# HGRN's input without the root in its elements, and the first two projection units run chunk by chunk while x is copied in

## The reference, cut to what matters

```
u = rmsnorm(x, norm_mix[0])            # x * rsqrt(mean(x*x) + eps) * gain
q, f, i, g = split(u @ w_in)           # 4 x 1024 columns
forget = lb + (1 - lb) * sigmoid(f);  key = 1 - forget
query = silu(q);  value = i;  log_f = log(forget)
# per head, in chunks: scores of query and key with decays from the
# running sum of log_f, a state carried from chunk to chunk,
o = rmsnorm(o, out_gain) * silu(g)
h = x + o @ w_out
```

## Time and profile before

| | |
|---|---|
| median of 3 runs | 2271.11 us (2269.19 to 2276.2) |
| the profiled execution | 2268.27 us |
| its span in the trace | 2266.5 us |
| TensorE busy (matmul) | 2180.3 us, 96% of the span |
| VectorE (DVE), ScalarE (ACT), GpSimd (POOL) busy | 1007.2, 872.8, 1175.6 us |
| mean granted clock of TensorE | 0.987 |

### The profile page before, as it was taken

How to read it: one execution, slowest core, us unless ns; L and a number is a source line. 1 busy time by engine, 2 the same in 40 slices (tenths; PEclk the granted TensorE clock), 3 DMA queues, 4 the chain that set the end, 5 groups by cost and what they waited for, 6 DMA issues and landing times. The chain is left out here.

```text
span 2266.5 us, 28352 instructions
## 1 busy us (share of the span) xinstructions
PE 2180.3 (96%) x10458; PEld 1795.5 (79%) x10458; DVE 1007.2 (44%) x1479; ACT 872.8 (39%) x1237; POOL 1175.6 (52%) x639
## 2 busy tenths in 40 slices
PE   4899999999999999989999999999899999999997
PEld 3788878888888978878888888788656888888886
DVE  5365566431434037754431446442675235422432
ACT  4567754221323223444221333434465234322222
POOL 3877855554565454535554555455113555554552
PEclk8999999999999999999999999999899999999999
DMA  3121213332332322223332332322101223332331
GB/s 135 56 65 56 74 47 93 93 109 86 95 108 85 93 85 67 72 70 102 94 112 83 93 107 88 123 63 90 56 14 51 95 93 93 100 110 80 101 104 72
DMA packets 53254, 193.30 MB, mean 85 GB/s; under 512 B 6816, under 2 KB 7728, under 8 KB 52912
## 3 DMA queue, kind: packets, MB, share of 16 engines
q1 hardware_dynamic: 50688, 184.95, 26.1%
q10 hardware_dynamic: 2480, 7.19, 0.8%
HBM read 187.92 MB, written 4.19 MB: 85 GB/s over the span
## 5 line engine op out<-in xcount | busy, mean ns | idle before, releaser
L1495 POOL TENSOR_TENSOR w_split<-ring,w_split 128x1024 fp32r<-128x1024 f32 (+3 forms) x327 | 842.9, 2578 | 857.1 <-ACT w_split L1013 857.1
L1013 ACT CAST w_split<-ring 128x1024 fp32r<-128x1024 f32 (+3 forms) x327 | 356.4, 1090 | 1018.2 <-PE ps L385 882.8
L383 PE MATMUL ps<-u_split,w_split 128*128 128x512 f32 x1768 | 705.8, 399 | 22.5 <-POOL w_split L1495 9.7
L385 PE MATMUL ps<-u_split,w_split 128*128 128x512 f32 x1768 | 693.3, 392 | 0.0
L384 PE MATMUL ps<-u_split,w_split 128*128 128x512 f32 x1768 | 692.9, 392 | 0.0
L383 PEld LDWEIGHTS ps<-u_split,w_split 128*128 128x128 f32 x1768 | 334.9, 189 | 102.0 <-issue 19.9
L385 PEld LDWEIGHTS ps<-u_split,w_split 128*128 128x128 f32 x1768 | 334.6, 189 | 71.5
L384 PEld LDWEIGHTS ps<-u_split,w_split 128*128 128x128 f32 x1768 | 335.0, 189 | 68.3 <-issue 1.2
L383 PE MATMUL ps<-hid,w_split 128*128 128x512 f32 x648 | 254.5, 393 | 4.2 <-DVE arena L1975 2.8
L384 PE MATMUL ps<-hid,w_split 128*128 128x512 f32 x648 | 253.3, 391 | 0.0
L385 PE MATMUL ps<-hid,w_split 128*128 128x512 f32 x648 | 253.1, 391 | 0.0
(11 more groups left out here) (297 smaller groups left out, 2535.6 us busy)
## 6 DMA issues: line engine op xcount, KB each, us to landing
ring<-in_w_hgrn SPq DMA_DIRECT2D x32, 512.0 KB, 3.6
ring<-in_w_attn_qk SPq DMA_DIRECT2D x24, 512.0 KB, 3.5
ring<-in_w_merge SPq DMA_DIRECT2D x24, 512.0 KB, 3.2
ring<-in_w_gu0a SPq DMA_DIRECT2D x22, 512.0 KB, 3.5
ring<-in_w_gu0b SPq DMA_DIRECT2D x22, 512.0 KB, 3.6
ring<-in_w_gu1a SPq DMA_DIRECT2D x22, 512.0 KB, 3.5
ring<-in_w_gu1b SPq DMA_DIRECT2D x22, 512.0 KB, 3.5
ring<-in_w_gu2a SPq DMA_DIRECT2D x22, 512.0 KB, 3.5
```

Source lines behind the costliest of these rows:

```text
L383: nc.tensor.matmul(ps[:, bank], ws[:, 0, r, w], act[:, 0, c], start=c == 0, stop=False)
L385: m = nc.tensor.matmul(ps[:, bank], ws[:, 1, r, w], act[:, 0, c], start=False, stop=c == n - 1)
L1013: nc.scalar.copy(ws[:, 0, slot, 0:w], ring[:, r, 0:w]).then_inc(s["w_hi"], 1)
L1495: nc.gpsimd.tensor_tensor(ws[:, 1, slot, 0:w], ring[:, r, 0:w], ws[:, 0, slot, 0:w].bitcast(F32), ALU.subtract).then_inc(s["w_lo"], 1)
```

## The change

The root is no longer in u: `first_norm` on ACT makes the high part of x times gain straight from x (Copy with a scale), `first_input` on DVE the low part, while the squares run beside. SP issues gains and lbl first, then the weights of units 0 and 1, then x with a semaphore for each pair of chunks, ones, and the rest. TensorE runs units 0 and 1 of head 0 in turn by chunks as they come, then the mean square, then goes on. The root is applied to each of the four results of every head by a product on DVE (`hgrn_raw`, from the bank to SBUF), so the sigmoids, the query and silu(g) now read SBUF, and ACT's copy of the value is gone. The third sigmoid moves beside the first two on ACT, silu(g) to behind the first masked score copy on DVE. POOL has no part of the first norm; its lists of splits and level products at the start are reordered. Some semaphores are merged (v_root and r_tok to `roots`, mix_* to `mix_steps`, rope_a_scaled to `rope_scaled`) without other work.

```diff
-            for c in range(DC):
-                sp.dma_start(h[:, c], a["x"][:, c]).then_inc(s["x_loaded"], 16)
-            for dst, name in constants[:2]:
-                sp.dma_start(dst[:], a[name]).then_inc(s["norm_consts"], 16)
...
-                    for k in range(RING):
+                    for dst, const in constants[:2]:
+                        sp.dma_start(dst[:], a[const]).then_inc(s["norm_consts"], 16)
+                    for k in range(2):
+                        sp.dma_start(ring[:, k, 0:width], w[k]).then_inc(w_ready[k], 16)
+                    for c in range(DC):
+                        sp.dma_start(h[:, c], a["x"][:, c]).then_inc(s[f"x_loaded{c // 2}"], 16)
+                    sp.dma_start(ones[:], a["ones"]).then_inc(s["norm_consts"], 16)
+                    for k in range(2, RING):
                         sp.dma_start(ring[:, k, 0:width], w[k]).then_inc(w_ready[k], 16)
...
 # TensorE
-            FREED = ("sig_f", "query", "silu_g", "vf_ready")
+            FREED = ("raw_f", "raw_q", "raw_g", "vf_ready")
...
-            pe.wait_ge(s["norm_consts"], 32)
+            for c in range(DC):
+                hgrn_project(0, 0, ready=u_chunk(0), part=(c, c + 1))
+                hgrn_project(0, 1, part=(c, c + 1))
+            pe.wait_ge(s["norm_consts"], 16 * 3)
             mean_square(0)
-            for k in range(4):
-                hgrn_project(0, k, ready=None if k else u_chunk(0))
+            for k in range(2, 4):
+                hgrn_project(0, k)
...
 # ACT
+            def first_norm():
+
+                act.wait_ge(s["norm_consts"], 16 * 2)
+                hi("hgrn", 0)
+                hi("hgrn", 1)
+                for c in range(DC):
+                    act.wait_ge(s[f"x_loaded{c // 2}"], 16 * 2)
+                    nc.scalar.activation(us[:, 0, c], h[:, c], ACT.Copy, scale=gains[:, 0, c:c + 1]).then_inc(s["u_hi"], 1)
+                    if c >= 4:
+                        act.wait_ge(s["sq_sum"], max(c - 4, 1))
+                    nc.scalar.activation(nsq[:, c % 4], h[:, c], ACT.Square).then_inc(s["sq_ready"], 1)
+                rms(0)
...
+            def hgrn_sigmoid(head, raw, src, dst, done):
+
+                act.wait_ge(s[raw], cnt(head, 1, 1))
+                nc.scalar.activation(dst, src, ACT.Sigmoid).then_inc(s[done], 1)
...
-            hgrn_sigmoid(0, 0, sf_, "sig_f")
-            hi("hgrn", 2)
-            hgrn_sigmoid(0, 1, sq_, "sig_q")
-
             act.wait_ge(s["lb_steps"], 5)
             nc.scalar.activation(lbt[:, 0:3], lbt[:, 0:3], ACT.Exp).then_inc(s["lb_steps"], 1)
+            hi("hgrn", 2)
+            hgrn_gate_sigmoids(0)
+            hi("hgrn", 3)
             hgrn_log(0)
-            hi("hgrn", 3)
+            hi("hgrn", 4)
             decay_exps(0, dec, 0)
             decay_exps(0, dec, 1)
-            hi("hgrn", 4)
             decay_exps(0, dec, 2)
+            hi("hgrn", 5)
             decay_exps(0, dec, 3)
             state_exps(0, bcum, dec, chd)
-            hi("hgrn", 5)
-            hgrn_value(0)
-            hgrn_sigmoid(0, 2, sg_, "sig_g")
...
                 if more:
-                    hgrn_sigmoid(nxt, 0, sf_, "sig_f")
-                    hgrn_sigmoid(nxt, 1, sq_, "sig_q")
+                    hgrn_gate_sigmoids(nxt)
+                hgrn_sigmoid(head, "raw_g", sgl, sg_, "sig_g")
                 act.wait_ge(s["vt_ps"], cnt(head, 1, 1))
...
-                    hgrn_value(nxt)
                     hi(*hgrn_unit(nxt2, 1)) if not isinstance(head, int) else hi("hgrn_out", 1)
-                    hgrn_sigmoid(nxt, 2, sg_, "sig_g")
...
 # POOL
-            lo("hgrn", 0)
-            norm(0, "hgrn")
-            lo("hgrn", 2)
-            lo("hgrn", 3)
-            hgrn_decayed(0, {4: lambda: lo("hgrn", 4), 8: lambda: lo("hgrn", 5)})
-            lo("hgrn", 6)
+            for k in range(5):
+                lo("hgrn", k)
+            hgrn_decayed(0, {2: lambda: lo("hgrn", 5), 5: lambda: lo("hgrn", 6)})
             lo("hgrn", 7)
...
 # DVE
+            def first_input(c):
+
+                dve.wait_ge(s["u_hi"], c + 1)
+                nc.vector.scalar_tensor_tensor(out=us[:, 1, c], in0=h[:, c], scalar=gains[:, 0, c:c + 1],
+                                               in1=us[:, 0, c].bitcast(F32), op0=ALU.mult, op1=ALU.subtract
+                                               ).then_inc(s["u_lo_odd"] if c % 2 else s["u_lo_even"], 1)
+                if c >= 2:
+                    add_square(0, c - 1)
...
+            def hgrn_raw(head, done, bank, dst):
+
+                unit = (1, 0, 2, 3).index(bank)
+                dve.wait_ge(s["w_used"], cnt(head, 4, FIRST["hgrn"] + unit + 1))
+                nc.vector.tensor_tensor(dst, ps[:, bank], rs[:], ALU.mult).then_inc(s[done], 1)
...
-                nc.vector.tensor_tensor(qry[x], sq_, ps[:, 0], ALU.mult).then_inc(s["query"], 1)
+                nc.vector.tensor_tensor(qry[x], sq_, qry[x], ALU.mult).then_inc(s["query"], 1)
...
-                nc.vector.tensor_tensor(sgl, sg_, ps[:, 2], ALU.mult).then_inc(s["silu_g"], 1)
+                nc.vector.tensor_tensor(sgl, sg_, sgl, ALU.mult).then_inc(s["silu_g"], 1)
...
-                    if n == 0:
-                        dve.wait_ge(s["scores"], cnt(head, 8, 1))
+                    if n == 1:
                         hgrn_silu(head)
...
                 if more:
                     end_exponents(bcum, dec)
+                    hgrn_raw(nxt, "vf_ready", 3, vf)
                 dve.wait_ge(s["o_lo"], cnt(head, 1, 1))
                 head_output(head, hgain, ors, otmp, sgl, otmp, s["o_full"])
+                if more:
+                    dve.wait_ge(s["o_scaled"], cnt(head, 1, 1))
+                    hgrn_raw(nxt, "raw_g", 2, sgl)
+                if not isinstance(head, int):
+                    hgrn_raw(nxt2, "raw_f", 1, sf_)
+                    output_rooted(head, ors, otmp, otmp, s["o_full"])
+                    hgrn_raw_query(nxt2)
```

More of the change, by code:

```diff
@@ L286, in program @@
         block = ctx.enter_context(nc.Block())
-        constants = ((gains, "gains"), (ones, "ones"), (ident, "ident"), (lvl_mask, "lvl_mask"), (reset, "reset"),
-                     (lbl, "lbl"), (hgain, "hgain"), (cos_a, "cos_a"), (sin_a, "sin_a"),
+        constants = ((gains, "gains"), (lbl, "lbl"), (ident, "ident"), (reset, "reset"), (lvl_mask, "lvl_mask"),
+                     (hgain, "hgain"), (cos_a, "cos_a"), (sin_a, "sin_a"),
                      (win_mask, "win_mask"), (res_mask, "res_mask"),
@@ L512, in hgrn_out @@
                 if lo == 0:
-                    pe.wait_ge(s[("query", "sig_f")[k]], HEADS_H)
+                    pe.wait_ge(s[("raw_q", "raw_f")[k]], HEADS_H)
                 unit("hgrn_out", k, hid, k, n=DC - 1, ready=lambda c: pe.wait_ge(s["o_lo"], c + 2), part=(lo, hi))
@@ L1145, in _, with hgrn_gate_sigmoids @@
             act.wait_ge(s["credit"], 2)
-            norm(0, "hgrn")
-            def hgrn_sigmoid(head, k, dst, done):
-                src = (1, 0, 2)[k]
-                act.wait_ge(s["w_used"], cnt(head, 4, FIRST["hgrn"] + k + 1))
-                if head != 0 and k:
-                    act.wait_ge(s[("", "query", "silu_g")[k]], cnt(later(head, -1), 1, 1))
-                nc.scalar.activation(dst, ps[:, src], ACT.Sigmoid).then_inc(s[done], 1)
+            first_norm()
+            def hgrn_sigmoid(head, raw, src, dst, done):
+                act.wait_ge(s[raw], cnt(head, 1, 1))
+                nc.scalar.activation(dst, src, ACT.Sigmoid).then_inc(s[done], 1)
+            def hgrn_gate_sigmoids(head):
+                hgrn_sigmoid(head, "raw_f", sf_, sf_, "sig_f")
+                hgrn_sigmoid(head, "raw_q", qry[(head if isinstance(head, int) else head[1]) % 2], sq_, "sig_q")
             def hgrn_log(head):
@@ L1819, in _ @@
             nc.vector.memset(start[:, 2:3], 0.0).then_inc(s["o_rstd"], 2)
-            for c in range(1, DC - 1):
-                add_square(0, c)
-            dve.wait_ge(s["norm_consts"], 32)
+            for c in range(DC):
+                first_input(c)
             def cumulate(it, b, log_decay):
@@ L2119, in times_sin @@
                 if x == 0:
[L2120 removed]
+                    dve.wait_ge(s["rope_scaled"], 4)
                 if x >= 2:
@@ L2346, in _ @@
             ffn(2, 7)
-            norm(7, s["credit"])
+            last_norm(7, s["credit"])
 def kernel(**inputs):
```

113 lines of the change are left out of this document (46 added, 67 removed).

## The result

Seven runs of each kernel: 2272.55 us before (2269.19 to 2277.68) and **2255.45 us after** (2253.3 to 2264.35). The ratio is 0.9928, with a 95% interval of 0.9907 to 0.9948: 17.1 us faster by the medians, where 2250 was forecast. The profiled execution of the changed kernel took 2261.79 us, its span is 2260.0.

The account below looks back on a forecast made before the run. TensorE, busy nearly all the span, was taken as the bound. Prologue -24.6 and heads +3.6 give -21.0 us: 2268.27 profiled becomes 2247.3, and the median, 2.8 above, 2250; range 2241 to 2260.

Parts of the forecast that it names:

- Steps 1 to 3: Prologue copies, weight splits and x parts: weights 0 and 1 split by 11.2 us, first low part held until then.
- Step 4: Prologue, units 0 and 1 in turn: 48 matmuls from 11.3 to 24.2 us, some 10 at 1.2 GHz.
- Step 5: Prologue, weight 2 split only after the root: TensorE waits 6.7 us, unit 2 then takes 7.4, to 40.0.
- Step 6: Prologue, units 3 to 5 run through in 16.3 us; head 0 starts at 56.3, 24.6 us gained, bounds 19 to 27.
- Head 0: First head: POOL a few microseconds behind its old place, but weights 6 and 7 and last levels still in time.
- Rival D: Heads: query and silu, reading SBUF, both stand out a POOL split; 4.6 us lost per head, 2278.7 us; chance 0.03.
- Heads 1 to 5: Head loop: scan to POOL's split 0.7 us later, less 0.1; TensorE waits 0.6 more per head, 3.6 in six.
- 0.1 of spare: Head loop: POOL ends the split about 0.1 us before TensorE starts that unit, taken off the 0.7 us delay.
- rival A: Heads: they lose nothing, as ACT's freed 3 us reach the loop and cover silu; 2245.5 us; chance 0.25.
- The sum: Whole kernel: prologue -24.6 and heads +3.6 give -21.0 us, 2250 for the median.

Follow-up runs that it names:

- second pair: Kernel before and changed kernel, unaltered, each traced once more on another chip: head 0 starts 24.3 us earlier in the changed one, the last head 16.9.
- POOL waits: Changed kernel, with POOL in head 0 waiting for the next head's key before its two end products: head 0 period 35.97 us, where it was 37.83.
- early, weight 5 too: Changed kernel, weights 2 and 3 cast before root's Ln, weight 5 cast and split earlier, POOL waiting for key in head 0: head 0 at 52.44, last head 284.39 us.
- silu between levels: Changed kernel, third sigmoid behind the log on ACT, silu between DVE's first and second pair of decay levels: head periods 35.1 to 37.1 us.
- both late: Changed kernel, third sigmoid behind the log on ACT and silu behind DVE's state chain: head period stays at 33.73 us.
- the last run: Changed kernel, weights 2 and 3 cast before root's Ln, POOL in head 0 waiting for key: 2252.96 us against 2274.97 for the kernel before, ratio 0.9911.

## Why the prediction was right, and where its steps were off

The forecast of 2250 lay 5.5 us low, inside its range. The mechanism of the start and of the later heads was the one that the trace shows; head 0 was missed, and two errors of the first steps cancelled. By its steps:

- **Steps 1 to 3** (copies, splits, x): TensorE starts at 11.03, predicted 11.3, but that is in part luck. ACT loads a table (1.28 us from 5.57) ahead of the casts, which the sum had not. The casts ended at 8.9, predicted 7.7, and POOL's splits at 10.3 and 13.1, predicted 8.6 and 11.2. The first low part was to stand out the split of weight 1 to 11.2. It stood out that of weight 0 instead and got in ahead of the other. That the gap is a matter of 0.1 us, and that TensorE starts 2.2 us later when it is missed, wasn't seen. DVE, then POOL of the changed kernel:

```profile
9.51 1.37 DVE L1702 SCALAR_TENSOR_TENSOR u_split<-arena,gains_sb,u_split 128x512 fp32r<-128x512 f32 x1 [8.42 <-ACT u_split L1046]
...
10.29 2.83 POOL L1504 TENSOR_TENSOR w_split<-ring,w_split 128x1024 fp32r<-128x1024 f32 x1
```

- **Step 4** (48 matmuls in turn): 26.07, predicted 24.2. The term mis-sized is the slow phase: 15 matmuls at 0.43 us, where 10 were reckoned from the earlier trace rows, and a wait of 0.52 for the late split of weight 1. The traces of the changed kernel and its variants have 9 to 17 slow matmuls here, so no single number would have done. From 18.46 on the matmuls are 0.23 us apart (the 47 in 10.60 us of the earlier trace rows give 0.2255, not 0.2265, a difference of no weight). The Trainium skill tells of one kernel whose cycling through banks kept bringing back the half clock (TensorE: Matmul & The Clock Gate, "A second HAM failure mode: psum-queue depth-cycling"); the trace of these turns between two banks shows no such fall after 18.46.
- **Step 5** (the hole): 6.2 us of waiting, 6.7 predicted. Unit 2 took 7.9 us, not 7.4, again by more slow matmuls.
- **Step 6** (units 3 to 5): they ran through, but for 0.37 us. Weight 4's split took 4.49 us beside DVE's level halves and ended at 47.8, predicted 43.5; the bounds had reckoned with such a split for weight 5. Head 0 at 59.0, predicted 56.3: 21.9 us gained (24.3 in the second pair), inside 19 to 27.
- **Head 0** is the step that failed. I wrote that POOL "is then a few microseconds behind its old place", and checked only whether its results come in time for TensorE. I did not ask which DVE instruction now stands beside POOL's end products and split. The forget product did: 5.41 us. Head 0 lost 4.7 us, of which 0.6 are the loss of every head and 4.1 are DVE's delay. "POOL waits" shows POOL's work beside DVE as the cause and takes 1.9 of them away; the rest moved to other instructions. Rival D described the mechanism, but for query and silu in every head.
- **Heads 1 to 5**: predicted 0.6 us each by TensorE's wait for POOL's split; measured 0.55, a wait of 0.47. The cause is also the one given. Without silu ahead of it the scan stays at +6.96, held by the log, and without silu and sigmoid it comes at +6.46. POOL's string starts 0.5 later, not 0.7, and next to nothing of the 0.1 of spare was there. The two table loads of a head that were to go went (7 to 5) and brought nothing, as said against rival A; by the periods A is out.
- **The sum**: -21.9 + 4.7 + 2.7 = -14.5 at the last head in the first pair of traces, -24.3 + 4.7 + 2.7 = -16.9 in the second, -17.1 by the medians of the whole. The forecast had -24.6 + 3.6 = -21.0: the start and head 0 make up the difference.

## What to carry to other kernels

Where one engine feeds another without slack, its whole unbroken string counts: an instruction of a third engine that slows one link by 0.5 us costs as much as a start that is 0.5 us late, so a moved instruction has to be checked against what the other engines run beside it, before and behind its new place. When a change starts a stage earlier, list what of the slower engines now falls on its first steps; the hole tends to come back a few units later. In a short prologue, what stands first in a list decides, not what lands first.

## What the runs showed of the hardware

- A DVE instruction can wait for more than one instruction of POOL: L1919, with one SBUF input, stood out four in a row (the rest of a half level, two products in 2.53, a split in 2.38), 5.41 us in all, and 0.65 where POOL waited for it. But it need not be so: in the prologue the low part issued at 9.51 was served between two splits that followed each other directly. It was done after 1.37 us, and the second split took 2.83 for 2.35. The Trainium skill (SBUF — State Buffer, "SBUF: two separate sides") says that who starts first has the pair of ports for the whole instruction; the trace agrees with that in both cases. Who gets in between two instructions of POOL stays open.
- At the first low part a few hundredths decided whether DVE got into the gap between two splits (issued at 10.10 it did, at 10.13 and 10.27 it did not); the price was 2.2 us of TensorE's start.
- In the first stretch (11.0 to 18.4 us) the profile's clock column shows 1.00 while the matmuls are 0.43 us apart. The column and the pace agree elsewhere (0.50 and 0.43 at 34 to 38 us); at the very start go by the starts of the matmuls.
- What an idle stretch of TensorE costs behind it differs from one time to the next. After 2.2 us without a matmul it ran at 1.2 GHz for 6.7 us ("early, weight 5 too"), and after 2.83 the clock fell in the kernel before. After 2.80 at the same place in the changed kernel, and after 2.38 in "silu between levels" (head at 101.21), it stayed at 1.00.
- One stretch of 650 matmul records had the clock at 1.00 and 111.8 us in one execution ("both late"), 0.90 and 122.3 us in another of nearly the same program (the last run). The 10.5 us between them are as much as the changed kernel's fastest and slowest runs differ by; which stretch made the slow ones slow isn't shown, since the fastest have no trace.
